# Streaming encoder step: parameter loads one visit earlier, squares ahead of the turned halves, first weights split

## What is computed

```
h = rms_norm(x, norm_g)
fq, fk, fv, fg, ff, su, sg, mq, mg = split_columns(h @ w_in)
logf    = log_sigmoid(ff + b_forget)
fox_out = fox_attend(rms_norm(fq), rms_norm(fk), fv, logf) * silu(fg)
ssm_out = s5_mixer(su, ...) * silu(sg)
mem_out = memory_attention(rms_norm(mq), mem_k, mem_v) * silu(mg)
y = x + concat([fox_out, ssm_out, mem_out]) @ w_out
```

## Time and profile before

| what | us |
|---|---|
| median of 3 runs | 1474.91 (1472.54 to 1475.08) |
| the profiled execution | 1476.74 |
| its span in the trace | 1475.0 |
| PE busy | 1409.9 (96%) |
| DVE busy | 931.6 (63%) |
| ACT busy | 736.7 (50%) |
| POOL busy | 282.3 (19%) |

### The profile page before, as it was taken

One profiled execution on the slowest core, in us unless ns is written; L12 is line 12 of the kernel. 1 busy time (PEld: TensorE's weight loads), 2 busy tenths in 40 slices (PEclk: granted clock), 3 DMA queues, 4 the chain that ended last, 5 costly groups with the idle time before them and its releaser, 6 DMA issues.

```text
span 1475.0 us, 28505 instructions
## 1 busy us (share of the span) xinstructions
PE 1409.9 (96%) x10126; PEld 1164.5 (79%) x10126; DVE 931.6 (63%) x1934; ACT 736.7 (50%) x1764; POOL 282.3 (19%) x344
## 2 busy tenths in 40 slices
PE   7999999999999989999999999999999999999998
PEld 7999767788877767777777888878888787778886
DVE  3589755692476787655334666666666566487785
ACT  5666423432443364435334776666777668621221
POOL 1111342100043342111001110101000003444542
PEclk9999999999999999999999999999999999999999
DMA  7786599986369588788984973470733702265552
GB/s 219 231 276 236 177 279 246 310 256 203 107 159 346 171 256 260 252 281 268 312 291 125 241 166 67 100 149 19 166 81 72 152 2 66 94 201 187 193 183 89
DMA packets 207613, 276.05 MB, mean 187 GB/s; under 512 B 49456, under 2 KB 146128, under 8 KB 203984
## 3 DMA queue, kind: packets, MB, share of 16 engines
q1 hardware_dynamic: 206432, 274.22, 64.1%
q10 hardware_dynamic: 1040, 0.00, 0.0%
HBM read 186.93 MB, written 86.00 MB: 185 GB/s over the span
## 4 chain that ended last, share of the span: by engine, by line
PE 55%; DVE 5%; issue 4%; ACT 3%; POOL 3%; DMA 1%; SPq 1%; ACTq 0%; DVEq 0%; POOLq 0%
PE in_g L924 13%; PE attn_pv L2485 9%; PE attn_s L2546 8%; PE attn_t L2469 8%; PE attn_s L2450 4%; PE attn_s L2453 3%; PE attn_pv L2546 3%; DVE attn_tops L2765 2%; ACT attn_probs L2579 1%; POOL in_hv L1796 1%; PE in_b L1099 1%; PE in_b L1051 1%; DVE attn_probs_turned L2778 1%; PE in_b L1154 1%; PE in_b L1119 1%
## 5 line engine op out<-in xcount | busy, mean ns | idle before, releaser
L924 PE MATMUL in_g<-in_wh,in_xh 128*128 128x512 f32 (+2 forms) x904 | 331.9, 380 | 11.5 <-DVE in_z L1535 5.5
L924 PE MATMUL in_g<-in_wl,in_xh 128*128 128x512 f32 (+2 forms) x904 | 321.8, 369 | 0.0
L2765 DVE TENSOR_REDUCE attn_tops<-attn_s 128x1 f32<-128x512 f32 (+3 forms) x288 | 175.4, 617 | 139.3 <-PE attn_s L2453 138.4
L2579 ACT ACTIVATE attn_probs<-attn_s,attn_negmax 128x512 f32<-128x512 f32 (+3 forms) x384 | 227.3, 603 | 23.8 <-DVE attn_negmax L2769 23.8
L924 PE MATMUL in_g<-in_wh,in_xl 128*128 128x512 f32 (+2 forms) x904 | 234.9, 379 | 1.5 <-DVE in_xl L1518 1.3
L2469 PE MATMUL attn_t<-all_ident,attn_probs 128*128 128x128 f32 x1216 | 192.2, 276 | 15.8 <-ACT attn_probs_turned L2589 8.7
L924 PEld LDWEIGHTS in_g<-in_wh,in_xh 128*128 128x128 f32 x904 | 165.5, 189 | 47.8 <-issue 16.8
L924 PEld LDWEIGHTS in_g<-in_wl,in_xh 128*128 128x128 f32 x904 | 165.6, 189 | 28.0
L2469 PEld LDWEIGHTS attn_t<-all_ident,attn_probs 128*128 128x128 f32 x1216 | 146.4, 142 | 50.3 <-ACT attn_probs L2579 16.8
L924 PEld LDWEIGHTS in_g<-in_wh,in_xl 128*128 128x128 f32 x904 | 158.0, 189 | 34.9 <-issue 5.2
L2485 PE MATMUL attn_pv<-attn_probs_turned,attn_v 128*64 128x128 f32 x2176 | 134.6, 275 | 0.0
(11 more groups left out here) (357 smaller groups left out, 2457.2 us busy)
## 6 DMA issues: line engine op xcount, KB each, us to landing
in_xu<-scratch_xt SPq DMA_DIRECT2D x87, 512.0 KB, 5.2
in_xl<-scratch_xt SPq DMA_DIRECT2D x34, 512.0 KB, 4.6
in_raw<-in_w_in SPq DMA_DIRECT2D x40, 256.0 KB, 5.7
scratch_xt<-in_xu SPq DMA_DIRECT2D x19, 512.0 KB, 5.3
scratch_xt<-in_xl SPq DMA_DIRECT2D x17, 512.0 KB, 6.1
scratch_k<-in_x_turned SPq DMA_DIRECT2D x17, 512.0 KB, 7.0
scratch_q<-in_x_turned SPq DMA_DIRECT2D x17, 512.0 KB, 5.5
in_x_turned<-in_x_prompt SPq DMA_DIRECT2D x16, 512.0 KB, 4.6
```

The lines of the kernel that those rows point to most:

```text
L924: last = X.matmul(g_ps[b][:, 0:m], x, ws[:, c, w0:w0 + m], start=(c == 0 and h == 0 and ws is wh), stop=(c == KC - 1 and h == 1))
L2579: last = F(probs[:, s % 2, i, at:at + n, :], s_ps[g % RING][:, at:at + n, :], ACT.Exp, bias=negmax[:, s % 2, top:top + 1], accum_out=total)
L2765: V.tensor_reduce(tops[:, s % 2, i:i + 1], bank[:, 0:n, :].rearrange("p n k -> p (n k)"), AX.X, ALU.max).then_inc(s_top, 1)
```

## The change

Three edits. The 14 parameter DMAs are put at visits 0 to 4, where they stood at visits 1 to 5. The square of tile j on ACT stands in front of the four copies of tile j, where it stood behind them; for tile 0 it stands behind the first three weight chunks. And for chunk 0 `wh` is made by ACT between the two halves of tile 0, and `wl` by DVE likewise, while the other seven chunks stay where they were. No instruction is added or taken away.

```
--- before.py
+++ after.py
@@ -146,7 +146,7 @@
 
 
     order = [("weights_in", 0, c) for c in range(KC)] + [
-        ("gains_in",), ("x", 0), ("weights", 0, 0), ("weights", 0, 1), ("weights", 0, 2)]
+        ("gains_in",), ("x", 0), ("weights", 0, 0), ("square", 0), ("weights", 0, 1), ("weights", 0, 2)]
     behind = list(behind)
     n_of = [sum(1 for w in visits[:v] if w[0] == p) for v, (p, _, _) in enumerate(visits)]
 
@@ -363,7 +363,7 @@
     decay_steps(late)
     sample_steps(late, 6)
     behind += [(pass_start["memkv" if n < 6 else "memq"] + (0 if n < 6 else 1), s) for n, s in enumerate(late.listed())]
-    beside = {(1 + n // 3, n % 3): [("parameters", n)] for n in range(14)}
+    beside = {(n // 3, n % 3): [("parameters", n)] for n in range(14)}
     gate = pass_start["gate"]
     beside[gate + 1, 1] = [("early_fill",)]
     for n in range(7):
@@ -1176,7 +1176,7 @@
                         act.wait_ge(s_norm, 16)
                     else:
                         act.wait_ge(s_gain, 16 * 6)
-                    for c in range(*PARTS[part]):
+                    for c in range(1 if (k, part) == (0, 0) else PARTS[part][0], PARTS[part][1]):
                         act.wait_ge(s_w[c], 16 * runs_upto[k + 1])
                         if k and part < 2:
                             act.wait_ge(s_wpart, 2 * (k - 1) + part + 1)
@@ -1184,6 +1184,12 @@
                             act.wait_ge(s_g, pass_start[p])
                         F(wh[:, c, 0:m], raw[:, c, 0:m], ACT.Copy,
                           scale=gains[:, int(p == "memkv"), c:c + 1]).then_inc(s_wh, 1)
+                if what == "square" or what == "x" and n[0]:
+                    j = n[0]
+                    act.wait_ge(s_x[j % 2], 16 * (j // 2 + 1))
+                    act.wait_ge(s_ssq, j)
+                    t = items[j][1]
+                    F(work[:, :], x_turned[:, j % 2, :], ACT.Square, accum_out=ssq[:, t:t + 1]).then_inc(s_ssq, 1)
                 if what == "x":
                     j = n[0]
                     if items[j][2] and item_visit[j] >= 2:
@@ -1198,10 +1204,11 @@
                         if items[j][2]:
                             F(xh[:, item_visit[j] % 2, 4 * h:4 * h + 4, :], xt_ps[h][:, :, :], ACT.Copy).then_inc(s_xth, 1)
                         F(xu[:, j % 2, 4 * h:4 * h + 4, :], xt_ps[h][:, :, :], ACT.Copy).then_inc(s_xu, 1)
-                    act.wait_ge(s_x[j % 2], 16 * (j // 2 + 1))
-                    act.wait_ge(s_ssq, j)
-                    t = items[j][1]
-                    F(work[:, :], x_turned[:, j % 2, :], ACT.Square, accum_out=ssq[:, t:t + 1]).then_inc(s_ssq, 1)
+                        if j == 0 and h == 0:
+
+                            act.wait_ge(s_norm, 16)
+                            act.wait_ge(s_w[0], 16)
+                            F(wh[:, 0, 0:WIDE], raw[:, 0, 0:WIDE], ACT.Copy, scale=gains[:, 0, 0:1]).then_inc(s_wh, 1)
                 if what == "split":
                     j = n[0]
 
@@ -1506,6 +1513,12 @@
                         dve.wait_ge(s_xu, 2 * j + h + 1)
                         V.tensor_tensor(xl[:, v % 3, 4 * h:4 * h + 4, :], xu[:, j % 2, 4 * h:4 * h + 4, :],
                                         fl(xh[:, v % 2, 4 * h:4 * h + 4, :]), ALU.subtract).then_inc(s_xtl, 1)
+                        if j == 0 and h == 0:
+
+                            dve.wait_ge(s_norm, 16)
+                            dve.wait_ge(s_wh, 1)
+                            V.scalar_tensor_tensor(wl[:, 0, 0:WIDE], raw[:, 0, 0:WIDE], gains[:, 0, 0:1], fl(wh[:, 0, 0:WIDE]),
+                                                   ALU.mult, ALU.subtract).then_inc(s_wl, 1)
                 if what == "split" and items[n[0]][0] in SPLIT:
                     j = n[0]
                     v = item_visit[j]
```

## The result

| what | before | after |
|---|---|---|
| median of 5 runs each, us | 1474.91 (1471.11 to 1475.62) | 1467.56 (1466.37 to 1468.84) |
| ratio, 95% interval | | 0.9943 [0.9923, 0.9964] |
| the profiled execution, us | 1476.74 | 1467.56 |
| its span, us | 1475.0 | 1465.9 |

The change makes the kernel 7.35 us faster, where 9.4 were forecast; the interval of the ratio reaches from 5 to 11 us.

A forecast was written before the change was run, and what follows sets the result against it. PE was taken as the bound, busy 96% of the span, losing time in waits for DVE's `z`. Gains of 1.7 + 6.35 + 1.5 = 9.5 us, taken as 1474.9 - 9.4, gave 1465.5 us, range 1462 to 1471.5.

The forecast's parts named there:

- First edit: Start, chunk 0 made between tile 0's halves: first product 1.99 us earlier, about 0.3 lost at chunk 1; gain 1.7 us.
- Second edit: State-pass visits, square ahead of the copies: visits 7.07 us apart instead of 7.47, waits for `z` shrink; gain 6.35 us.
- Third edit: State pass, parameter DMAs one visit earlier: `log_dt` is there ahead of its use; gain 1.5 us.
- The wait at 50.54: PE's wait in the state pass, 1.27 us shown, 1.50 lost, put down to ACT waiting 4.23 us for `log_dt`.
- The price of 0: Small DMAs ahead of tile loads on SP: 2 to 3 us of cover, cost taken as 0, bound 3 us.
- some 1.7 us of cover: ACT's 3.18 us hole ahead of the copies keeps this much spare once it holds the square.
- Everything behind 142 us moves as a block.: From the first keys product on, PE's later waits come earlier by the same amount, so the gain stays whole.
- Rival 3: Later passes: the gain is given back by a stretch tied to transfers; gain under 2.9 us, 1473.5 us; 8%.
- 1: Late visits: DVE becomes the bound and most of the 0.40 us losses stay; gain 6.5 to 7.5, 1468 us; 12%.
- 2: Start or parameters give nothing: clock rises late, a tile load comes late; gain 4 to 6, 1470 us; 9%.
- 5: Start: the clock rises sooner; gain 11.5, 1463.4 us; 8%.
- 4: SP's queue: loads of items 4 to 7 land late behind parameter DMAs and hold ACT; slower, 1478.5 us; 3%.

The follow-up runs named there:

- e1: The kernel before with only the square moved ahead of the copies; 1470.45 us in one execution, then timed at 1466.99 us, ratio to before 0.9953.
- e4: The changed kernel with the parameter DMAs back at visits 1 to 5, so square and split only; 1467.27 us in one execution.
- e9: The changed kernel plus 15 idle start transposes, a later output-stage load of x, and chunk 1 also made between tile 0's halves; 1458.90 us, ratio 0.989.
- e11: e9 with only the first four parameter DMAs one visit early, the others back where before had them; 1465.61 us, ratio to before 0.9912.
- e6: The changed kernel with the output stage's 1 MB load of x moved behind the next mix tile's loads on SP; 1463.19 us, ratio to before 0.9908.
- e7: The changed kernel plus 15 idle identity transposes on PE at the start; 1462.74 us, ratio to before 0.9899.
- e8: The changed kernel with the additions of e6 and e7 together; 1459.73 us, ratio to before 0.9895.
- e10: e9 with all 14 parameter DMAs back at visits 1 to 5; 1461.13 us, ratio to before 0.99.

## Why the prediction was right, and where not

- **The time.** 1465.5 was forecast, 1467.56 measured, 2.1 us more and inside the range of 1462.0 to 1471.5. The forecast gain of 9.4 us lies inside the measured interval of 5 to 11. (The terms add up to 9.55; nothing hangs on it.) Two misses of opposite sign lie under it: K came 1.1 us earlier than the 133 forecast, and 2.8 us were given back behind the last score.
- **What bounds the kernel.** Right: PE's waits for `z` were the loss, and ACT's square lay in the chain that made them.
- **First edit.** P0 8.40 forecast, 8.43 measured; chunk 1 at 10.0, measured 9.92. Gain 1.7, and 1.7 between the means of six executions, within 1 us of spread. The prediction booked all of P0's 1.96 us with the split. The edits share it: the square alone gives 1.0 (e1 has P0 at 9.35 and 9.45, since the square of tile 0 had stood ahead of the first weight), the split alone 1.8 of P0 but 1.0 of S1, for then the square stands ahead of chunk 1.
- **Second edit.** The cadence of 7.07 us and the waits that vanish are as forecast, and a last wait stays (131.86, 0.42 us for about 0.6). The size isn't: 6.35 us forecast, 7.6 measured (122.80 - 115.17 of e1 timed).
- **Third edit.** This term failed: 1.5 us forecast, 0.05 measured beside the other two (e4 against after), 0.44 alone. The step "The wait at 50.54 ... hangs on ACT standing until 44.90 for `log_dt`" is true of before, but the wait was treated as separate from the second edit, whose list of waits left it out. The loads wait for the squares, so the second edit brings `log_dt` 3.5 us nearer and PE only 1.6: the wait goes by that alone. So the 1.5 us came, but from the second edit, and the sum of both, 7.85, met 7.77. That the sum fitted was not proof of its terms; e4 and e1 timed showed this.
- **SP's queue.** The load of item 4 was issued at 23.55, forecast 23.5. That of item 5 was issued at 31.68 and there at 39.4, not near 38, and PE wanted it at 39.5, not 40.6: the cover was 0.1 us where 2 to 3 were forecast. The price of 0 held, but by luck; 0.9 us of earlier start used it up (e9). The "some 1.7 us of cover" of the square in ACT's hole was 0.17 us at that tile, too.
- **"Everything behind 142 us moves as a block."** Wrong as a sentence: 10.6 us at K, 11.9 at the last score, 9.1 at the end. "PE's later waits are for DVE and ACT" overlooked PE's wait for POOL ahead of `attn_out`, which is a wait for SP's small loads, and the clock that falls behind it; it overlooked the pauses in the attention stage as well, which before and after both have. Rival 3 had the mechanism (a stretch tied to transfers) but for the gain as a whole; of 10.6 us, 1.5 went, and as far as the other kernels' pauses tell, that was chance.
- **Rivals.** 1 didn't occur: the visits that were 7.47 us apart are 7.07 apart. 2's half on the parameters did. 5, the early rise of the clock, came half true in the profiled execution (S1 16.83, and 17.38 to 17.91 in the three others with that start). 4's mechanism is real: e11 is that rival, with an issue of 8.65 us and a tile load 1.10 us late, but in the change as made it didn't decide.

## What to carry to other kernels

Where two edits shorten the same chain, price them together: ask of each wait what it would be after the other edit, and run the pair with one taken away. A small load's place in a queue has a value that depends on how early the rest of the program is, so look again at the queue each time a stretch gets faster. And a gain at the start should be followed to the last pause of the bounding engine; here the order of one queue 1,280 us later was worth 3.4 us of its own stretch, beside 7.4 for the whole change. Last, when a time moves more than the marks do, find the stretch in which the rest lies before you book it with the edit: in e6 and e7 some of the gain lay in the attention stage, which neither edit touches.

## What the runs showed of the hardware

- A pause of PE costs more than it shows when the clock falls behind it: 1.28 us idle cost 1.15 in e1 and left the pairs at 0.40, 2.91 us idle cost 4.3 in e11 with pairs of 0.64 behind it, and 4.1 us in the output stage was followed by a mean granted clock of 0.85 over 20 us.
- The length of a pause alone doesn't decide whether the clock falls: in after PE stood 2.24 us up to 975.7 and the granted clock behind it is 1.00 (976 to 984), and it stood 1.98 us up to 1157.5 and the clock behind it is 0.75, then 0.64 (to 1163).
- PE can stand 0.7 to 2.8 us for nothing that the profile shows ("issue"). It did so once or twice in the attention stage of all nine kernels without the idle transposes at the start, and in none of the five with them.
- Transposes against the identity raise the clock: in e8, e9 and e10 the seven idle ones ran 1.37, 1.29 and 1.06 us where they took 1.70 in e7 and e11, ahead of any product.
- At the start the granted clock reads 1.00 where pairs take 0.64 us (after, 8 to 12 us), so there the durations tell the level and the clock column doesn't. Later the column tells it: 0.54 for such pairs in e11 (55.7 to 58 us).
- The time to issue one small DMA on SP differs with what was issued ahead of it: 2.05 us in e9 and 8.65 us in e11 for the same `b_im`, in e11 behind a load and two stores of 512 KB.
